# Second attention computed token by token, its weights turned by products with the unit matrix, and matmuls of the stages around it moved into its loop

## What is computed

```python
x = x + s5_mixer(rms(x))                 # state-space layer, ends in val * sigmoid(gate), the "GLU"
x = x + conv_ffn(rms(x)); x = x + sigmoid(rms(x) @ w_gate) * (p @ w_proj)
k, v = shared_kv(x)                      # k: head norm over 64; v: 8 heads of 128
q = head_norm((rms(x) @ w_q)), 8 heads, 2 halves of 64 each
for each head, each block of 128 queries:
    s[c] = q[c] @ k[c].T / 8 + bias(distance), causal, c = 0, 1
    attn = softmax(s[0]) - lam * softmax(s[1])
    o = attn @ v
x = x + (rms_per_head(o) * subln * (1 - lam_init)) @ w_o
x = x + conv_ffn(rms(x)); x = x + sigmoid(rms(x) @ w_gate) * (p @ w_proj)
```

## Time and profile before

| what | value |
| --- | --- |
| median of 3 runs | 2135.4 us |
| the profiled execution, whole | 2137.13 us |
| its span | 2135.3 us |
| TensorE busy | 96% of the span |
| VectorE, ScalarE, GpSimd busy | 58%, 38%, 22% |
| mean granted TensorE clock | 0.974 |

### The profile page before, as it was taken

The page is one execution under the profiler, slowest core; times in us unless marked ns, Lnnn a source line. Parts: engine busy times, 40 slices in busy tenths (PEclk is TensorE's granted clock), DMA queues, the critical chain, the costliest instruction groups (busy, mean ns, idle before and its releaser), DMA issues.

```text
span 2135.3 us, 26693 instructions
## 1 busy us (share of the span) xinstructions
PE 2039.7 (96%) x9714; PEld 1621.7 (76%) x9714; DVE 1230.0 (58%) x1695; ACT 816.9 (38%) x1248; POOL 465.5 (22%) x626
## 2 busy tenths in 40 slices
PE   8999999999999879999999989999888999999988
PEld 7998678888887767877878877655564877877877
DVE  5345365656355984577365557533485577365555
ACT  4323242222135874344243335322364444243333
POOL 3110039998814551000000011011100100000010
PEclk9999799999999999999999999999897999999999
DMA  4221023264442422222223232211100222223232
GB/s 144 90 80 61 20 89 109 89 217 150 167 160 81 156 84 89 89 89 92 95 98 109 75 103 99 82 62 62 50 26 20 79 89 98 90 98 109 79 99 99
DMA packets 54866, 201.69 MB, mean 94 GB/s; under 512 B 6438, under 2 KB 6950, under 8 KB 53740
## 3 DMA queue, kind: packets, MB, share of 16 engines
q1 hardware_dynamic: 47132, 166.39, 23.1%
q0 software_dynamic: 7632, 33.91, 4.4%
HBM read 184.51 MB, written 15.77 MB: 94 GB/s over the span
## 4 chain that ended last, share of the span: by engine, by line
PE 86%; DVE 9%; ACT 2%; issue 1%; DMA 1%; POOLq 0%; POOL 0%; SPq 0%; DVEq 0%; ACTq 0%
PE ps L440 69%; PE ps L612 6%; PE ps L763 2%; PE ps L572 1%; PE ps L838 1%; PE ps L554 1%; DVE t L1793 1%; PE ps L1769 1%; DVE w_lo L426 1%; DVE t L1429 1%; DVE rstd L535 0%; DVE t L564 0%; PE ps L794 0%; PE ps L1760 0%; DVE pp L1609 0%
## 5 line engine op out<-in xcount | busy, mean ns | idle before, releaser
L440 PE MATMUL ps<-x_hi,w_hi 128*128 128x512 f32 x1280 | 512.4, 400 | 2.7 <-DVE w_lo L426 2.6
L440 PE MATMUL ps<-x_lo,w_hi 128*128 128x512 f32 x1280 | 507.8, 397 | 0.0
L440 PE MATMUL ps<-x_hi,w_lo 128*128 128x512 f32 x1280 | 505.4, 395 | 0.0
L426 DVE TENSOR_TENSOR w_lo<-raw,w_hi 128x1024 fp32r<-128x1024 f32 x308 | 401.6, 1307 | 173.0 <-ACT w_hi L422 172.7
L422 ACT ACTIVATE w_hi<-raw 128x1024 fp32r<-128x1024 f32 x308 | 321.7, 1048 | 216.3 <-DMA raw<-in_wstream 143.6
L440 PE MATMUL ps<-a_hi,w_hi 128*128 128x512 f32 x864 | 345.1, 399 | 10.7 <-DVE pp L1609 4.8
L440 PE MATMUL ps<-a_lo,w_hi 128*128 128x512 f32 x864 | 342.5, 396 | 0.0
L440 PE MATMUL ps<-a_hi,w_lo 128*128 128x512 f32 x864 | 342.5, 396 | 0.0
L440 PEld LDWEIGHTS ps<-x_hi,w_hi 128*128 128x128 f32 x1280 | 241.5, 189 | 83.9 <-issue 22.9
L440 PEld LDWEIGHTS ps<-x_hi,w_lo 128*128 128x128 f32 x1280 | 241.7, 189 | 55.7
L440 PEld LDWEIGHTS ps<-x_lo,w_hi 128*128 128x128 f32 x1280 | 241.4, 189 | 55.1 <-issue 1.2
(11 more groups left out here) (364 smaller groups left out, 2544.6 us busy)
## 6 DMA issues: line engine op xcount, KB each, us to landing
raw<-in_wstream SPq DMA_DIRECT2D x308, 512.0 KB, 3.3
ev<-mix_ev POOLq DMA_DIRECT2D x8, 1024.0 KB, 5.1
mix_cp<-c_p POOLq DMA_DIRECT2D x8, 640.0 KB, 3.5
cp<-mix_cp POOLq DMA_DIRECT2D x8, 640.0 KB, 6.3
mix_ev<-v_b POOLq DMA_DIRECT2D x8, 512.0 KB, 3.5
fall<-fall POOLq DMA_DIRECT2D x4, 544.0 KB, 5.1
h<-in_xT SPq DMA_DIRECT2D x4, 528.0 KB, 7.2
mix_ev<-e_r POOLq DMA_DIRECT2D x1, 2048.0 KB, 8.5
```

Of the source, the lines that this page charges most:

```text
L426: e.tensor_tensor(w_lo[:, u.slot, :], raw[:, u.c % 2, :], w_hi[:, u.slot, :], ALU.subtract)\
L440: last = e.matmul(ps[:, bank, :], wt[:, u.slot, w], x[:, k0 + k, 0:SEQ], start=(k == 0 and n == 0), stop=(k == kt - 1 and n == 2))
```

## The change

- GLU: `glu_open_pe` multiplies the first six of eight input tiles of GLU units 0 and 1 before the last mixer step on TensorE, those of units 2 and 3 behind it, and `glu_close_pe` adds the last two tiles of all four; the splits of units 2 and 3 move ahead of the last mixer step on ScalarE and VectorE.
- q, k and v are computed with tokens on the partitions, in six groups of 512 features (`group_pe`): the inputs are the stationary operand and the weights the moving one, 96 matmuls of 512 columns a group. The DMA brings four pieces of 128 x 256 for each unit (`load_columns`). ScalarE evicts (`group_act`, a copy with the token norm, and a square for q and k); VectorE sums the squares and multiplies by reciprocals of 128 x 32. Groups 0 to 3 (q, first half of k, first half of v) run ahead of the attention, groups 4 and 5 inside it.
- No fences. The loop has 37 steps i and starts each head with the block of N = 512. Next to scores, turn and product with the values, TensorE turns q (steps with i mod 4 = 1), k (2) and the finished output o (3) of a head through one PSUM bank, 7; ScalarE and VectorE split them out of it. `FILL` puts 16 halves of groups 4 and 5 (12 matmuls each) and 8 halves of the first half of the output projection into 24 of the steps.
- The mixed weights are not divided by the first sum; the head norm of o is corrected for it (`dve_out`), with a square root on ScalarE for each head (`act_root`).
- The mixed weights are turned by a product with the unit matrix `ident`, keys and values then both having tokens on the partitions; the transposes of the values are gone. Scores have three PSUM banks in rotation in place of four, turned weights one in place of two.
- Behind the loop: `out2_pe` for the second half of the output projection.

The diff, cut to its core:

```diff
+    def glu_open_pe(e, s):
+        u = Unit(U_GLU + s)
+        e.wait_ge(lo_ok, u.n(1))
+        e.wait_ge(unit_ev, U_GLU)
+        if s >= 2:
+            e.wait_ge(v_ev, KT)
+        for k in range(GLU_K):
+            if s == 0:
+                e.wait_ge(g_lo, k + 1)
+            product(e, u, s, a_hi, a_lo, k, KT)
...
+    def glu_close_pe(e, s):
+        u = Unit(U_GLU + s)
+        for k in range(GLU_K, KT):
+            if s == 0:
+                e.wait_ge(g_lo, k + 1)
+            last = product(e, u, s, a_hi, a_lo, k, KT)
+        last.then_inc(unit_mm, 1)
...
+    FILL = {}
+    for k, i in enumerate((0, 1, 2, 3, 5, 6, 7, 8)):
+        FILL[i] = ("group", 4, k)
+    for k, i in enumerate((9, 10, 12, 13, 14, 16, 17, 18)):
+        FILL[i] = ("group", 5, k)
+    for k, i in enumerate((21, 22, 23, 25, 26, 28, 30, 32)):
+        FILL[i] = ("out", k // 2, k % 2)
+    SPLIT_AT = {}
+    for i, (kind, a, b) in FILL.items():
+        if kind == "group" and b >= 4:
+            SPLIT_AT[i + 1] = U_Q + 4 * a + b
+        elif kind == "out" and b == 1:
+            SPLIT_AT[i + 1] = U_WO + 4 + a
...
+        w = KT * P // count
+        src = A["wstream"][first * P:(first + count) * P, lo:lo + w].rearrange("(a p) c -> p a c", p=P)
+        e.dma_start(raw[:, n % 2, :].rearrange("p (a c) -> p a c", a=count), src).then_inc(raw_in[n % 2], 16)
...
+    def group_pe(e, g, half):
+
+        s, c = half // 4, half % 4
+        n = U_Q + 4 * g + c
...
+                o = ps[:, group_bank(g, tb), :].rearrange("p (a c) -> p a c", a=4)
+                r = slice(tb * P, (tb + 1) * P)
+                for i, (x, w) in enumerate(((hi, w_hi), (lo, w_hi), (hi, w_lo))):
+                    last = e.matmul(o, x[:, k, r], w[:, n % 4, :].rearrange("p (a k c) -> p k a c", a=4, k=2)[:, k % 2],
+                                    start=(k == 0 and i == 0), stop=(k == KT - 1 and i == 2))
...
+    def group_act(e, g, tb):
+
...
+        src, r = ps[:, group_bank(g, tb), :], rstd[:, tb:tb + 1]
+        ins = e.activation(group_store(g, tb), src, ACT.Copy, scale=r)
+        if g in NORMED:
+            k = 4 * NORMED[g] + tb
+            ins.then_inc(qn_c, 1)
+            ge(e, qn_s, k - 1)
+            ins = e.activation(sq[:, k % 2, 0:SEQ], src, ACT.Square, scale=r)
+        ins.then_inc(unit_ev, 1)
...
+    def turn_pe(e, kind, p):
+
+        k = TURN[kind, p]
+        if k == 0:
+            e.wait_ge(tab_ok, 2)
+        ge(e, tr_ev, k)
+        if kind == "o":
+            e.wait_ge(oy_ok, p + 1)
+            for qt in range(4):
+                last = e.matmul(ps[:, 7, qt * P:(qt + 1) * P], o_held(p)[:, qt, :], flip[:, :], start=True, stop=True)
...
+            for tb in range(4):
+                last = e.transpose(ps[:, 7, tb * P:(tb + 1) * P], group_store(g, tb)[:, (p % 4) * P:(p % 4 + 1) * P],
+                                   ident[:, :])
+        last.then_inc(tr_mm, 1)
...
+    def turn_act(e, kind, p):
+        hi, lo, src, gain = turn_at(kind, p)
+        e.wait_ge(tr_mm, TURN[kind, p] + 1)
+        e.activation(hi, src, ACT.Copy, scale=gain).then_inc(tr_hi, 1)
+
+    def turn_dve(e, kind, p):
+        hi, lo, src, gain = turn_at(kind, p)
+        e.wait_ge(tr_hi, TURN[kind, p] + 1)
+        e.scalar_tensor_tensor(lo, src, gain, hi, ALU.mult, ALU.subtract).then_inc(tr_ev, 1)
...
+        for g in range(4):
+            if who == "pe":
+                for half in range(8):
...
+                    e.wait_ge(lam_v, 1)
+                    e.matmul(ps[:, 7, 0:2], ones[:, :], small[:, 0, 0:2], start=True, stop=True).then_inc(lam_mm, 1)
+                    e.wait_ge(lam_a, 1)
+                    e.wait_ge(tab_in, 16)
+                    e.matmul(ps[0:8, 6, :], rel[:, :], onehot[:, 0:SEQ], start=True, stop=True)
+                    e.matmul(ps[0:8, 7, 0:P], rel[:, :], onehot[:, SEQ:640], start=True, stop=True).then_inc(tab_mm, 1)
+            elif who == "act":
+                if g == 0:
...
+                for tb in range(2):
+                    group_act(e, g, tb)
...
+                for c in range(4):
+                    split_hi(e, Unit(U_Q + 4 * g + 4 + c))
+                for tb in range(2, 4):
+                    group_act(e, g, tb)
+                if g in NORMED:
+                    head_roots_act(e, g)
+                if g == 0:
+                    e.wait_ge(lam_mm, 1)
+                    e.activation(small[:, 1, 0:2], ps[:, 7, 0:2], ACT.Exp).then_inc(lam_a, 1)
...
+                e.wait_ge(unit_ev, U_Q + 16)
+            ge(e, nb_ok, 2 * g - 1)
+            for n, (a, b) in enumerate(((qr_hi, kr_hi), (qr_hi, kr_lo), (qr_lo, kr_hi))):
...
+            ge(e, pt_ok, g)
             for j in range(qt + 1):
-                last = e.matmul(ps[:, 4 + sl, j * P:(j + 1) * P], ST[g % 3][:, 0, j * P:(j + 1) * P], flip[:, :],
+                last = e.matmul(ps[:, 5, j * P:(j + 1) * P], ST[g % 3][:, 0, j * P:(j + 1) * P], ident[:, :],
                                 start=True, stop=True)
...
+                e.wait_ge(unit_ev, U_Q + (16 if g == 0 else 24))
             for j in range(qt + 1):
-                last = e.matmul(ps[:, 6 + p % 2, qt * P:(qt + 1) * P], vtok[:, p % 2, j, :], pt2[:, sl, j, :],
+                last = e.matmul(ps[:, 6, 0:P], PT2[g % 2][:, j * P:(j + 1) * P], v_tok[:, j, p * P:(p + 1) * P],
                                 start=(j == 0), stop=(j == qt))
...
         def dve_mix(g):
-            N = (g % 4 + 1) * P
...
-            n = dve.did(e.tensor_scalar(t[:, 0, 0:N], t[:, 0, 0:N], small[:, 3, k:k + 1], None, ALU.mult))
+            n = dve.did(e.scalar_tensor_tensor(small[:, 3, k + 1:k + 2], col(15, g), lam_pair[:, 1:2], small[:, 3, k:k + 1],
+                                               ALU.mult, ALU.mult))
             e.wait_ge(dve_did, n)
             e.scalar_tensor_tensor(t[:, 0, 0:N], t[:, 1, 0:N], small[:, 3, k + 1:k + 2], t[:, 0, 0:N],
                                    ALU.mult, ALU.add).then_inc(nrm_ok, 1)
 
+        def dve_hold(g):
+            p, qt, N = step(g)
+            e.wait_ge(pv_mm, g + 1)
+            if g % 4 == 0 and p >= 2:
+                e.wait_ge(tr_mm, TURN["o", p - 2] + 1)
+            e.tensor_copy(o_held(p)[:, qt, :], ps[:, 6, 0:P]).then_inc(od_ok, 1)
...
+            r = slice(4 * p, 4 * p + 4)
+            e.wait_ge(os_ok, 4 * p + 4)
+            n = dve.did(e.scalar_tensor_tensor(small[:, 0, 0:4], state[:, 15, r], eps_o[:, 0:1], state[:, 15, r],
+                                               ALU.mult, ALU.mult))
+            e.wait_ge(dve_did, n)
+            e.scalar_tensor_tensor(state[:, 13, r], state[:, 12, r], 1.0 / (P * (1.0 - LAM) ** 2), small[:, 0, 0:4],
+                                   ALU.mult, ALU.add).then_inc(ov_ok, 1)
+            e.wait_ge(or_ok, p + 1)
+            n = dve.did(e.reciprocal(state[:, 14, r], state[:, 13, r]))
+            e.wait_ge(dve_did, n)
+            e.wait_ge(od_ok, 4 * p + 4)
+            o = o_held(p)
+            e.tensor_tensor(o, o, state[:, 14, r].unsqueeze(2).to_broadcast([P, 4, P]), ALU.mult).then_inc(oy_ok, 1)
...
+        def act_root(p):
+            r = slice(4 * p, 4 * p + 4)
+            e.wait_ge(ov_ok, p + 1)
+            e.activation(state[:, 13, r], state[:, 13, r], ACT.Sqrt).then_inc(or_ok, 1)
...
+        def turns(i, turn):
+            if i % 4 == 1 and i < 28:
+                turn(e, "q", i // 4 + 1)
+            if i % 4 == 2 and i < 28:
+                turn(e, "k", i // 4 + 1)
+            if i % 4 == 0 and i >= 8:
+                turn(e, "o", (i - 8) // 4)
...
             if who == "pe":
-                if g < 32:
-                    if g % 4 == 0:
-                        pe_values(g // 4)
-                    pe_scores(g)
-                if 2 <= g < 34:
-                    pe_turn(g - 2)
-                if g >= 3:
-                    pe_pv(g - 3)
...
+                if i < 32:
+                    pe_scores(i)
+                if i < 28 and i % 4 in (1, 2):
+                    turn_pe(e, "qk"[i % 4 - 1], i // 4 + 1)
+                if 2 <= i < 34:
+                    pe_turn(i - 2)
+                if fill and fill[0] == "group":
+                    group_pe(e, fill[1], fill[2])
+                elif fill:
+                    out2_pe(e, fill[1], fill[2], (0, 1, 2, 3))
+                if 3 <= i < 35:
+                    pe_pv(i - 3)
+                if i % 4 == 3 and 7 <= i < 35:
+                    turn_pe(e, "o", (i - 7) // 4)
+            elif who == "act":
+                if 4 <= i < 36:
+                    act_square(i - 4)
+                if i < 32:
+                    act_exp(i)
+                if 2 <= i < 34:
+                    act_turn(i - 2)
+                if i % 4 == 3 and i >= 7:
+                    act_root((i - 7) // 4)
+                turns(i, turn_act)
+                if done and done[0] == "group" and done[2] % 4 == 3:
+                    for tb in (done[2] // 4 * 2, done[2] // 4 * 2 + 1):
```

(30 more changed lines are left out.)

578 lines of the change are left out of this document (316 added, 262 removed).

## The result

The kernel after takes 2107.2 us (median, 2104.8 to 2111.2), the kernel before 2136.6 beside it: a ratio of 0.9865, with a 95% interval of 0.9845 to 0.9884. The gain is 29 us. The forecast was 61 and its range ended 3 us lower. The profiled execution of after took 2107.52 us (span 2105.7), 31.4 more than the 2076.1 that the sum gave for it.

What follows compares the result with a forecast made beforehand. The prediction took TensorE as busy 96% of the span, but VectorE as setting the second attention's loop. Terms -9 - 95.1 + 100.2 - 57.1 = -61.0 took 2137.13 to 2076.1, median forecast 2074.5 us; own range 2054 to 2100.

Steps and rivals of the forecast that it cites:

- Step 1: Mixer's end and GLU: 36 matmuls fill TensorE's 9.1 us hole, 36 follow; -9 us (-14 to -4).
- term for the splits of unit 4: GLU: unit 4's splits stand behind ScalarE's first sigmoid, table load and next inputs, costing about 4.4 us.
- Step 2: q, k, v, from group 0 to the first scores: 105.4 us in place of 200.5, -95.1.
- The wait for lam: After group 0 TensorE waits for lam's exponential on ScalarE, 7 us, then 1 of table products; +8 (bounds 2 and 10).
- The turns: In q, k, v, ahead of the loop: turns of head 0, +1 us.
- Step 3: Attention loop: 87.8 becomes 188 us, +100.2, set by serial links between engines; bounds 150 and 215.
- Step 4: Head norm of o and output projection: 27.1 goes whole, 22.5 in place of 52.5; -57.1 us.
- A: Loop: TensorE sets it, loads and links hide under fills, 158 us; whole time 2044.5; chance 0.18.
- B: Loop: a table change costs twice 1.28, sixteen changes nearly all on the links; +20, 2095 us; chance 0.12.
- C: Loop: TensorE stays at 1.2 GHz, loop 290 us, whole time 2177, slower; chance 0.04.
- D: Whole change: product with ident no faster than with flip, group order and fills bring nothing; 2135 us; chance 0.01.
- E: Weight loads for q, k, v: 1 KB pieces load at half the rate; +16, 2090 us; chance 0.03.

Runs made afterwards that it cites:

- the third try: Against the kernel after: unit 4's last-head products before half of unit 5's, each next feed-forward split behind its pair of tiles; 2105.3 us, ratio 0.9861.
- The edit of the root: Against the kernel after: ScalarE's square root for each head's o replaced by eight tiny VectorE operations (two Newton steps); 2103.6 us, ratio 0.9847.

## Why the prediction was wrong, by its own steps

**Step 1, GLU, failed: 2 in place of 9.** It took the first six input tiles as ready when the hole of 9.1 us opens. The earlier trace rows show how long the hole is, and nothing of what is in memory then; VectorE begins the sixth low part at 795.04 in after (and in before at 794.12, a row that the prediction didn't look for), so in both kernels it comes after the hole. The hole could take 30 matmuls (five tiles, two units), not 36. With five, about 4.4 us came back; what holds the other 2.6 stays open (the third unit's wait of 1.96 us stands there, and no run takes it out). Its term for the splits of unit 4 was right in kind and too high: 2.89 where 4.4 was given. (14 less 4.4 is 9.6, which it wrote as 9.)

**Step 2, q, k, v, mis-sized: 115.8 in place of 105.4.** The wait for lam was described link by link, and it measured 6.16 of stop and 2.3 of table products, 8.5 against 8. What was not there is a stop inside group 0. The chain of waits of after:

```profile
1335.48 0.75 DVE a_lo L550
1336.23 1.15 DVE small L2472
1337.38 1.14 DVE w_lo L428
...
1338.56 8.17 PE ps L1729 x24
```

TensorE runs the first halves of the group's first two weight units, 24 matmuls, up to 1333.4. The third unit's low part stands on VectorE's list behind all eight low parts of the inputs and lam's product, so TensorE stands 5.17 us and then runs 24 matmuls in 8.17 in place of 5.6: 7.7 us, present in the diff's lists and not priced. Before, the first unit took its input tiles one by one and waited 3.1 us for the last two, and the old 200.5 had that in it; the new sum had nothing in its place. The turns, given 1 us, cost 4.9: 2.3 of wait, 1.0 of their own, and 1.6 because the 12 matmuls behind took 4.42 in place of 2.8. The clock behind lam's stop, given 3, cost 1.9 (12 matmuls in 4.66), and the scores waited 2.55 where 3 was given. Together 7.7 + 0.5 + 3.9 - 1.1 - 0.4 = 10.6, against the 10.4 missed. The experiments took lam's stop and the turns out; for the stop in group 0 no repair was tried, and it is read from the traces alone.

**Step 3, the loop: 189.7 against 188, right in its main claim, and in its sum partly by luck.** Right: no engine is busy throughout, links between the engines set it, and the turns of q and o hold TensorE in five of the last six heads. But of the 35.4 us for which TensorE stands in the loop these turns are 16.9, and the longest single stop, 5.2, is elsewhere. TensorE's longest groups of waits in the loop of after (total, times, longest):

```profile
PE ps L1729 <- ACT sq L1750: 6.9, 2, 5.2
PE ps L1783 <- DVE rstd L2027: 6.9, 2, 4.0
PE ps L1783 <- DVE rt L2027: 5.2, 2, 2.7
PE ps L1788 <- DVE o_lo L1811: 4.6, 2, 2.6
PE ps L1977 <- DVE rstd L2011: 4.3, 3, 2.3
PE ps L1977 <- ACT v_tok L1745: 4.0, 1, 4.0
```

L1783 is the turn of o (12.1 us in all), L1788 the turn of q that waits for o's split. Not priced were the first and last rows: group 4's second half and the first product with group 5's values wait 6.9 and 4.0 for evictions that stand far down ScalarE's list. Between the first scores of one head and the next the prediction had 20, 22, 26.5, 22.7, 23.5, 22.2 and 22.2 us, and 29 for the last head and the end. After has 17.8, 20.5, 32.5, 26.6, 23.9, 20.2, 20.9 and 27.2. The third and fourth head, where group 4 ends and group 5 runs, took 9.9 more, and the six others together 8.4 less: the sum came out because these misses cancel. TensorE's own sum was 145 and it is 154, with parts at half clock (0.78 from 1485 to 1513). Too high were VectorE (117, measured 111) and ScalarE (128, measured 113.5). And one statement doesn't hold: that a load starts only when its wait is over. On ScalarE in after:

```profile
1564.00 1.28 ACT L2034 ACT_TABLE_LOAD   x1
1566.91 0.72 ACT L2034 ACTIVATE t<-t,small 128x512 f32<-128x512 f32 x1 [1.63 <-DVE small L1990]
```

The load is over 1.6 us before the exponential can start, so the return to the exponential's table is hidden here. What the earlier trace rows showed at 1531.31 is one load that came after a wait, not a rule. But it is hidden in some heads only. Of the seven returns in the loop three end before the exponential starts (by 2.61, 1.63 and 0.67 us), and behind the four others it starts 0.01 us later; three of these, at 1482.54, 1507.21 and 1586.20, stand in the chain of waits with their full 1.28. The chain's rows for the last:

```profile
1586.20 1.28 ACT L2034
...
1587.49 0.02 ACT t L2034
```

All seven changes to the root's table lie on the chain too. The edit of the root takes out seven changes and six returns. Nine of these 13 loads, 11.5 us, are on the chain, and the loop became 7.5 shorter; the rest went to whatever was next late. So the 188 was met partly because hidden loads and other terms priced too high stood against evictions and half clock not priced at all.

**Step 4, the tail, mis-sized: 46.2 in place of 35.95.** The window from 1644.9 to 1697.4 was taken as the output projection, 192 matmuls, and half of it, 22.5, left in place of 52.5. But 192 x 0.234 is 44.9, and the earlier trace rows has 217 records in it: one is of the statistic, and the other 24 matmuls (5.6 us) are the next feed-forward's, in front of it. They moved with the end and did not go away. The output matmuls and the turn of o took 24.7 us where 22.5 was given: 0.9 for the turn, 1.3 with a clock of 0.93. Some 2.3 more lie between them and the statistic, about the 2.2 that the third try got back. With the 5.6 that is 10.1, about the miss. "The start of the next feed-forward keeps its form: 0" was thus wrong, and the row's count could have shown it; that head 7's chain is hidden under 36 matmuls was right.

**Rivals.** A (TensorE sets the loop, 158) falls with the loop's 189.7 and with the products left out. (Against A it counted five steps without a fill; the list leaves seven, 11, 15, 19, 20, 24, 27 and 31.) B (a change of table costs twice 1.28) falls: a load starts 0.02 us after the operation before it and the activation can follow at once (1363.55 + 1.28, then 1364.84). And 13 changes less gave 7.5 us, where 13 x 2.56 would be 33, though part of them is hidden. By the Trainium skill (ScalarE: Activation LUTs, What ACT_TABLE_LOAD costs) there are 1.38 us of drain beside the load; no row here has them. C (1.2 GHz throughout) falls with a clock of 0.92, though it was the right worry in small: each of the four stops of 5 us or more in the changed stages is followed by several us at half clock (granted 0.65, 0.69, 0.57 and 0.71 in the 6 to 8 us behind them), and leaving work out of the fills lowered the clock from 0.92 to 0.85. The Trainium skill (TensorE: Matmul & The Clock Gate, Part 4: PE-mode transpose) says that transposes don't count as work for the clock; with 80 of them in place of products the loop's clock was 0.89, one hundredth under what the loops with products show (0.90 to 0.92), and the time the same. One execution can't tell whether that hundredth is theirs. D and E fall: q, k, v fell by 85 us, and no dense matmul of groups 1 to 3 waits for its weights.

The forecast's case, a loop set by links, was the right one to choose; what failed are the terms around it. Its own range of 2054 to 2100 was made of the loop's bounds and a few us for the rest, and the three other terms all missed to the same side, by 28 us together.

## What to carry to other kernels

Before work is put in a hole, look up when each of its inputs is written and count only what is ready: one tile too many held up the step that the hole was waiting for, by 9 us. Before a stage is priced at "half of its window", count the window's instructions against the stage's own; what is left over belongs to a neighbour and stays. When an operation is moved ahead or a group is opened at once, read the list of the engine that feeds its first instruction: a stop of 5 to 6.5 us cost TensorE its length and then some 2 to 2.5 us more, for 12 to 24 matmuls partly at half clock.

## What was not expected of the hardware

- A table load can run ahead of the wait of its activation (1564.00, the activation at 1566.91). It did so to some use in three of the loop's seven returns, and stood in the way in full in three.
- VectorE's low part of an input (L550) took 0.75 us alone and 1.18 beside GpSimd's sums, and GpSimd's sum 1.29 alone and 1.55 to 1.72 beside VectorE.
- A transpose of a 128 x 128 tile is one record of 297 ns, the product with the unit matrix two of 294; with 80 tiles TensorE's busy time differs by 5 us, and the time doesn't.
